# A two-layer mixer and expert kernel: scaled triangles and decay differences on ScalarE, an own region for the boundary factors, two weight items ahead of the transposes back, and another order at the start of the queries

## The chip, the cores and the metric

The kernel runs on one core of a Trainium2 chip. The metric is the device time of one execution in microseconds (us), median of several runs. The engines are PE (TensorE), VectorE (DVE), ScalarE (ACT), Pool (GpSimd) and SP (SyncE, which here only issues weight transfers).

## The reference, cut to what matters

Two blocks follow each other on x of 256 tokens by 1024 features. Each has a mixer and then a retrieval over 16384 single-neuron experts, of which every token takes 16 for each of 8 heads. The change is in the second block's mixer and at the start of both retrievals:

```
proj = _rmsnorm(x, norm1) @ w_in          # a_q a_k a_v a_beta a_alpha a_gate b_f b_i b_q b_gate g_a g_b
qkv  = silu(causal_conv(a_q, a_k, a_v))
beta = sigmoid(a_beta);  g = -exp(a_log) * softplus(a_alpha + dt_bias)
G = cumsum(g);  decay = where(causal, exp(G_i - G_j), 0)
lhs = eye + tril((k*beta) @ k^T * decay, -1)      # solved, unit diagonal
a_qk = (q @ k^T) * decay                          # o_a = gated delta rule
f_gate = lb + (1 - lb) * sigmoid(b_f)             # second recurrence, per-feature decay
y = sigmoid(g_a) * (o_a @ w_branch_a) + sigmoid(g_b) * (o_b @ w_branch_b);  x += y @ w_out

q = h2 @ w_pq;  s = q . sub_keys;  top 16 of each half, top 16 of the 256 sums -> expert index, gate
u = expert_u[idx]; h = gelu(x . u);  v = expert_v[idx];  x += sum(gate * h * v)
```

## The kernel before, in words

**Weights.** All weights stream as blocks of 128 x 1024 floats (512 KB) through `ring` (4 slots), in the order of `plan`. A block is two pieces of 512 columns. For each piece ScalarE writes the high part, rounded to fp32r (`ahead`, L903), then VectorE (L1283) or Pool (L2134) writes the residual; `by_pool` says which. There are six slots for split pieces (`PARTS`), so piece p waits until PE has used piece p - 6. Every engine's `ahead(n)` moves its own high-water mark by n pieces, at a place written by hand into that engine's program. PE's products are three fp32r matmuls (L357 to L359) a tile; 48 of them use four pieces and make one item (`by_feature` or `by_token`) in one of 8 PSUM banks.

**Order.** Every engine's program is written out by hand, and each engine takes its own strictly in order, with waits on semaphores. The second mixer has these stretches:

1. 12 conv items. VectorE applies the taps (L1818, L1821) and the second half of silu (L1832, L1834), ScalarE the tanh (L1152). In between step by step (`delta_gates`): the gates `beta` and `g`, the cumulated `G`, 16 triangles `TG` = triangle times g of one head (VectorE, L1796), ones times `TG` on PE (`("D", q)`, L662, four of them), the differences to `G` cut at zero (VectorE, L1802), the exponential (ScalarE, L1145) and the masking with the triangle (VectorE, L1807).
2. Item `ag0`, the `qk` transposes (L677) and their copies, then items `ag1` to `ag3` on PE while VectorE takes the sums of squares (L1858, L1860), ScalarE their root (L924) and VectorE scales q, k and v (`unit`, L1869 to L1873).
3. The transposes back (`("back", c2)`, L688) and their copies, the products `L` and `Q` (L705), which VectorE multiplies with the decays (L1882, L1884), item `bf0`.
4. The triangular inverse, six levels of four groups, 24 steps: L732 and L741 on PE, VectorE and ScalarE evacuate, L697 transposes. Items `bf1`, `bf2` and `bf3` lie between the steps. The items that follow are listed in `fillers`.
5. U (L760), the gated delta output, the second recurrence, the branches' outputs, `w_out2` and the residual.

**Experts** (`experts(e, ...)`, e = 1 and 2). PE makes query items from `wq`. Item i is copied by ScalarE (L914) and multiplied with the keys (`keyed`, L581); ScalarE scales the result into S (L1034). VectorE finds a head's 16 experts in `chosen(j)` (L1556 to L1606), which gives `eidx`. Pool gathers for each of 256 k one row pair for every token (L2156, 1 MB each, 10 landing slots). VectorE forms `dot(k)` (L1630) with the normed input, which `with_gain` (L1622) writes to PSUM. ScalarE makes gelu, weight and a diagonal (L1045 to L1053), PE adds the weighted rows (L604). The keys and two rows of gains come by DMAs that Pool issues (L2146 to L2149).

Of the kernel before, what the change touches and what calls it, by code (L numbers as in the profile page):

```python
# [14 lines left out]
P = 128  # L15
# [10 lines left out]
NLEV = 7  # L26

# [51 lines left out]
def build(nc, d, out):  # L79
    ctx = ExitStack()  # L80
    with ctx:
# [142 lines left out]
        BF = region(2048, 2048, c=8)  # L224
# [11 lines left out]
        SS = region(26624, 1024, h=8)  # L236
        WT = region(27648, 1024, h=8)
# [3 lines left out]
        bkf, bff, bqf = region(10240, 2048), region(2048, 2048), region(4096, 2048)  # L241
        BB, BFs, bb = spare[:, :].rearrange("p (s n) -> p s n", s=16), region(2048, 2048, s=16), spare[:, :]
# [88 lines left out]
        def tensor_program(pq, pe):  # L331
# [307 lines left out]
            def delta_gates():  # L639
# [16 lines left out]
                yield  # L656
                yield
                yield
                for q in range(4):
                    o = bank(("D", q))  # L660
                    pq.wait_ge(*on(("TG", 15)))
                    pe.matmul(o[:, :], ones, TG[:, 4 * q:4 * q + 4, :], start=True, stop=True).then_inc(*full(("D", q)))  # L662
                    yield
# [45 lines left out]
            def items():  # L709
                for name, i in fillers:  # L710
                    if name in ("bf", "bq"):
                        yield by_feature, (name, i), "w_in2", "n1"
                    elif name == "ya":
                        yield by_token_whole, (name, i), "wa", "oT", oT
                    else:
                        yield by_token, (name, i), "w_in2", "n1"
            left = items()

            def item():
                kind, *a = next(left)  # L720
                kind(*a)

# [170 lines left out]
        def scalar_program(aq, ac):  # L893
# [229 lines left out]
            def delta_gates():  # L1123
                copy(region(8192, T)[0:16], pb[place["ab"]][0:16, 0:T], "ab")
                yield
                abp = pb[place["abT"]][:, 0:32].rearrange("p (t n) -> p t n", t=2)
                aq.wait_ge(*full("abT"))
                ac.activation(v2(sv["beta"]), abp[:, :, 0:8], ACT.Tanh, scale=0.5).then_inc(*up("a_delta", "beta_tanh"))
                aq.wait_ge(*on("alpha_min"))
                ac.activation(sv["t2"], sv["t2"], ACT.Exp).then_inc(*up("a_delta", "alpha_exp"))  # L1130
                aq.wait_ge(*on("alpha_one"))
                ac.activation(sv["t2"], sv["t2"], ACT.Ln).then_inc(*up("a_delta", "alpha_ln"))
                aq.wait_ge(*on("ld_rows"))
                ac.activation(small[:, 320:328], r_alog, ACT.Exp).then_inc(*up("a_delta", "a_exp"))
                yield
                yield
                aq.wait_ge(*on("G_left"))
                ac.activation(sv["kd"], sv["kd"], ACT.Exp).then_inc(*up("a_delta", "kd"))
                ac.activation(sv["eG"], sv["G"], ACT.Exp).then_inc(*up("a_delta", "eG"))
                yield  # L1140
                yield
                for _ in range(4):
                    yield
                aq.wait_ge(*on(("taken", ("D", 3))))
                ac.activation(DT, DT, ACT.Exp).then_inc(*up("a_delta", "D_exp"))  # L1145

            def conv_tanh(i):
                aq.wait_ge(*on(("conv", i)))
                if i >= 4:
                    aq.wait_ge(*on(("silu", i - 4)))  # L1150
                tm = tmpc[:, (i % 4) * 512:(i % 4 + 1) * 512].rearrange("p (c t) -> p c t", c=2)
                ac.activation(tm, CT[:, 2 * i:2 * i + 2, :], ACT.Tanh, scale=0.5).then_inc(*up("a_conv", ("conv_tanh", i)))  # L1152

            gate_steps = delta_gates()
            for i in range(12):
                ahead(4)
                if i:
                    conv_tanh(i - 1)
                next(gate_steps, None)
            conv_tanh(11)  # L1160
            for _ in gate_steps:
                pass
            ahead(4)
            copy(AG[:, :, 0:T], half(("ag", 0)), ("ag", 0))
            for n, (g, t) in enumerate((g, t) for g in range(6) for t in range(NT)):
                if n % 2 == 0:
                    copy(QK[:, t, 4 * g:4 * g + 4, :], bank4(("qk", g, t)), ("qk", g, t))
            ahead(4)
            copy(AG[:, :, T:2 * T], half(("ag", 1)), ("ag", 1))
            root(nrm, "unit")  # L1170
            for i in range(2, 4):
                ahead(4)
                copy(AG[:, :, i * T:(i + 1) * T], half(("ag", i)), ("ag", i))
            for c2 in range(0, 12, 2):
                copy(CT[:, 2 * c2:2 * c2 + 2, :], half(("back", c2)), ("back", c2))
            aq.wait_ge(*on("lb_less"))
            ac.activation(p2, p2, ACT.Exp).then_inc(*up("a_lb", "lb_exps"))
            for i in range(4):
                aq.wait_ge(*on(("taken", ("ag", i))))
            ac.activation(gate_a, AGf, ACT.Tanh, scale=0.5).then_inc(*up("a_tanh", "ag_tanh"))  # L1180

# [23 lines left out]

            item()
# [3 lines left out]
            for n, (lev, g) in enumerate(steps):  # L1210
                if (4 * lev + g) % 8 == 7:
                    item()
# [60 lines left out]
        def vector_program(vq, ve):  # L1273
# [266 lines left out]
            def experts(e, wq):  # L1540
# [123 lines left out]
                ahead(4)  # L1664
# [98 lines left out]
            def delta_gates():  # L1763
# [30 lines left out]
                vq.wait_ge(*on("g"))  # L1794
                for s in range(16):
                    ve.tensor_scalar(TG[:, s, :], triu, sv["g"][:, s:s + 1], None, ALU.mult).then_inc(*up("v_delta", ("TG", s)))  # L1796
                    if s % 8 == 7:
                        yield
                for q in range(4):
                    vq.wait_ge(*full(("D", q)))  # L1800
                    for s in range(4 * q, 4 * q + 4):
# [45 lines left out]
            for _ in gate_steps:  # L1847
                pass
# [460 lines left out]
```

## Time and profile before

| what | value |
|---|---|
| median of 3 runs | 2039.79 us (2035.16 to 2040.49) |
| the profiled execution: its time, its span | 2036.71 us, 2034.9 us |
| PE busy, mean granted clock | 1702.4 us (84%), 0.973 |
| VectorE, ScalarE, Pool busy | 1336.4 us (66%), 913.9 us (45%), 839.4 us (41%) |
| chain that ended last | PE 38%, DMA 34%, DVE 16%, ACT 8% |
| first gather of experts 1 and 2 | 180.5 us, 1369.0 us |

The span runs from the first to the last instruction. A busy time is a sum over stretches with different limits. The chain follows each wait back to what ended it, and a granted clock of 1.0 is 2.4 GHz, 0.5 is 1.2 GHz.

### The profile page before, as it was taken

Reading aid. Unit: us, or ns where it says so; the run is one execution under the profiler, and the core shown is the slowest. Engines: PE = TensorE matmul, PEld = TensorE weight load, DVE = VectorE, ACT = ScalarE, POOL = GpSimd, SP = SyncE. Lnnn points to the kernel's source line nnn. Section 1 sums busy time; section 2 is a strip of 40 time slices with the busy share of each in tenths; the row PEclk is TensorE's granted clock in tenths of the full one; section 3 lists DMA queues with packets and bytes.
Section 4 is the critical chain, followed back from the end, with each engine's and each line's share of the span. In section 5 each row is a group of like instructions: output and inputs, shape, how many; then the busy total and the mean of one; then the engine's idle time right before and its main releaser. Section 6 shows DMA issues by size and latency. Waiting matters only on the chain.

```text
span 2034.9 us, 22626 instructions
## 1 busy us (share of the span) xinstructions
PE 1702.4 (84%) x7622; PEld 1047.5 (51%) x7622; DVE 1336.4 (66%) x2922; ACT 913.9 (45%) x2366; POOL 839.4 (41%) x762
## 2 busy tenths in 40 slices
PE   8986889877887778789799989977899787777887
PEld 7985444422322222579799989973444222222222
DVE  4666776766776664499646773547776677667644
ACT  5554545444544443445324344454444444444443
POOL 4325333333333333367525465544333333333331
PEclk9998999999999999999899999989999999999999
DMA  7446999999999999543213333559999999999996
GB/s 247 129 129 267 420 421 421 422 421 421 422 421 421 421 421 422 216 135 125 73 53 101 100 112 114 167 169 421 421 421 421 421 422 422 421 422 421 421 422 286
DMA packets 102052, 637.60 MB, mean 313 GB/s; under 512 B 11264, under 2 KB 12544, under 8 KB 36144
## 3 DMA queue, kind: packets, MB, share of 16 engines
q0 software_dynamic: 75216, 543.73, 64.3%
q1 hardware_dynamic: 26720, 92.43, 14.1%
q8 instruction: 60, 0.98, 0.2%
q14 instruction: 56, 0.46, 0.1%
HBM read 635.07 MB, written 1.05 MB: 313 GB/s over the span
## 4 chain that ended last, share of the span: by engine, by line
PE 38%; DMA 34%; DVE 16%; ACT 8%; issue 3%; POOL 0%; SPq 0%; DVEq 0%; ACTq 0%
DMA arena<-in_uv,arena 29%; PE pb L604 19%; DMA spare<-in_uv,arena 4%; PE pb L357 4%; PE pb L358 4%; PE pb L359 4%; ACT arena L1053 3%; DVE arena L1630 3%; PE pb L430 1%; PE pb L741 1%; ACT parts L903 1%; PE pb L732 1%; DVE arena L1821 1%; DVE parts L1283 1%; DMA arena<-in_sk 1%
## 5 line engine op out<-in xcount | busy, mean ns | idle before, releaser
L604 PE MATMUL pb<-arena 128*128 128x512 f32 x1848 | 910.2, 622 | 223.9 <-ACT arena L1053 222.0
L1630 DVE SCALAR_TENSOR_TENSOR arena<-arena,pb 128x1024 f32<-128x1024 f32 x462 | 563.3, 1219 | 375.2 <-DMA arena<-in_uv,arena 375.2
L2156 POOL DMA_INDIRECT arena<-in_uv,arena x462 | 438.3, 949 | 734.0 <-PE pb L604 681.9
L604 PEld LDWEIGHTS pb<-arena 128*128 128x128 f32 x1848 | 321.8, 192 | 779.3 <-ACT arena L1053 511.3
L2134 POOL TENSOR_TENSOR parts<-ring,parts 128x512 fp32r<-128x512 f32 x228 | 340.1, 1510 | 346.3 <-ACT parts L903 344.0
L1045 ACT ACTIVATE arena<-arena 128x1 f32<-128x1 f32 x512 | 103.3, 202 | 621.7 <-DVE arena L1630 567.3
L903 ACT ACTIVATE parts<-ring 128x512 fp32r<-128x512 f32 x328 | 197.8, 627 | 198.8 <-PE pb L359 183.2
L1053 ACT ACTIVATE arena<-cst,arena 128x128 f32<-128x128 f32 x512 | 205.5, 401 | 48.7 <-ACT arena L1048 1.1
L357 PE MATMUL pb<-xl,parts 128*128 128x256 f32 x704 | 221.6, 315 | 4.1 <-DVE xl L1315 2.6
L358 PE MATMUL pb<-xh,parts 128*128 128x256 f32 x704 | 201.3, 286 | 0.0
L359 PE MATMUL pb<-xh,parts 128*128 128x256 f32 x704 | 201.1, 286 | 0.0
L357 PE MATMUL pb<-parts,xh 128*128 128x256 f32 x608 | 176.7, 291 | 14.2 <-DVE parts L1283 9.6
L358 PE MATMUL pb<-parts,xl 128*128 128x256 f32 x608 | 174.2, 287 | 0.0
L359 PE MATMUL pb<-parts,xh 128*128 128x256 f32 x608 | 174.1, 286 | 0.0
L1048 ACT ACTIVATE arena<-arena 128x1 f32<-128x1 f32 x512 | 150.8, 294 | 19.3 <-ACT arena L1045 0.4
L1283 DVE TENSOR_TENSOR parts<-ring,parts 128x512 fp32r<-128x512 f32 x100 | 78.2, 791 | 104.3 <-ACT parts L903 104.1
L357 PEld LDWEIGHTS pb<-xl,parts 128*128 128x128 f32 x704 | 137.2, 195 | 16.4 <-issue 13.8
L358 PEld LDWEIGHTS pb<-xh,parts 128*128 128x128 f32 x704 | 137.3, 195 | 10.8 <-issue 10.8
L359 PEld LDWEIGHTS pb<-xh,parts 128*128 128x128 f32 x704 | 136.9, 195 | 0.0
L357 PEld LDWEIGHTS pb<-parts,xh 128*128 128x128 f32 x608 | 118.9, 196 | 15.1 <-DVE parts L1283 10.0
L358 PEld LDWEIGHTS pb<-parts,xl 128*128 128x128 f32 x608 | 119.0, 196 | 0.0
L604 PE MATMUL pb<-spare,arena 128*128 128x512 f32 x200 | 99.6, 621 | 23.2 <-ACT arena L1053 23.1
(297 smaller groups left out, 1779.2 us busy)
## 6 DMA issues: line engine op xcount, KB each, us to landing
ring<-in_w_in SPq DMA_DIRECT2D x108, 512.0 KB, 3.5
ring<-in_wq SPq DMA_DIRECT2D x32, 512.0 KB, 6.1
ring<-in_w_out SPq DMA_DIRECT2D x16, 512.0 KB, 3.6
arena<-in_uv,arena POOLq DMA_INDIRECT x462
ring<-in_wa SPq DMA_DIRECT2D x8, 512.0 KB, 3.4
ring<-in_wb SPq DMA_DIRECT2D x8, 512.0 KB, 3.8
arena<-in_sk POOLq DMA_DIRECT2D x2, 1024.0 KB, 6.3
arena<-in_tail POOLq DMA_DIRECT2D x1, 1280.0 KB, 11.3
```

The costliest lines, as they stand in the source:

```text
L357: pe.matmul(o, lh, rl, start=start, stop=False, skip_group_check=True)
L358: pe.matmul(o, ll, rh, start=False, stop=False, skip_group_check=True)
L359: return pe.matmul(o, lh, rh, start=False, stop=stop, skip_group_check=True)
L604: ins = pe.matmul(ys[hf][:, :], diags[:, k % 4, :], lands[k % LANDS][:, D + hf * 512:D + (hf + 1) * 512], start=k % (8 * K) == 0, stop=k % ...
L903: ac.activation(split(p)[0], raw(p), ACT.Copy).then_inc(*up("a_hi", ("hi", p)))
L1045: ac.activation(acted[:, k:k + 1], hidden[:, k:k + 1], ACT.Gelu).then_inc(*up("a_gelu", ("gelu", e, k)))
L1048: ac.activation(weight_of[:, k:k + 1], acted[:, k:k + 1], ACT.Copy, scale=gate[:, k:k + 1]).then_inc(*up("a_weight", ("weight", e, k)))
L1053: ac.activation(diags[:, k % 4, :], ident, ACT.Copy, scale=weight_of[:, k:k + 1]).then_inc(*up("a_diag", ("diag", e, k)))
L1283: ve.tensor_tensor(lo, raw(p), hi.bitcast(F32), ALU.subtract).then_inc(*up("v_lo", ("lo", p)))
L1630: ve.scalar_tensor_tensor(z, z, 1.0, xg[t], ALU.mult, ALU.mult, accum_out=hidden[:, k:k + 1]).then_inc(*up("v_dot", ("dot", e, k)))
L2134: gp.tensor_tensor(lo, raw(p), hi.bitcast(F32), ALU.subtract).then_inc(*up("g_lo", ("lo", p)))
L2156: gp.indirect_dma_start(lands[k % LANDS], None, rows_uv, bass.IndirectOffsetOnAxis(ap=eidx[:, k:k + 1], axis=0)).then_inc(*up(f"dma_rows{k ...
```

## The change

- The 16 triangles are made by ScalarE (`ACT.Copy` with a scale pointer), in four portions of the conv loop. The four D matmuls move from the conv loop to behind `ag1`. ScalarE reads the differences from PSUM as relu(G - D), in two batches (`decay_gaps`), and the exponential has scale -1. The root for `unit` stands behind the second batch and the copy of `ag2`, the exponential behind it. The masking multiply stands behind VectorE's copies of the transposes back.
- `BF` has a region of its own, apart from `CT`; `SS`, `WT`, `EX[0]` and `KW[1]` get other places.
- `EARLY = 2` items (`bf0`, `bf1`) go ahead of the transposes back, on all engines. The small constants of the lower bound (L1890 to L1900) and their exponential move into the end of the conv stretch. In the inverse one item is left (`n == 7`). Pool makes the four `silu` of the gate behind three items.
- Queries: VectorE splits 6 instead of 8 pieces ahead, runs `chosen(0)`, then `with_gain(0)` and `gates(0)`, then splits 6 instead of 4. Pool's mark ahead of the keys' DMA stands two pieces earlier.

```diff
+EARLY = 2
-        BF = region(2048, 2048, c=8)
+        BF = region(26624, 2048, c=8)
-        SS = region(26624, 1024, h=8)
-        WT = region(27648, 1024, h=8)
+        SS = region(28672, 1024, h=8)
+        WT = region(29696, 1024, h=8)
-        EX = [region(2048, 2048), region(30720, 2048)]
+        EX = [region(26624, 2048), region(30720, 2048)]
-        KW = [region(20480, 2048), region(26624, 2048)]
+        KW = [region(20480, 2048), region(2048, 2048)]
...
 # tensor_program
             for i in range(1, 4):
                 by_token(("ag", i), "w_in2", "n1")
+                if i == 1:
+                    for q in range(4):
+                        o = bank(("D", q))
+                        pq.wait_ge(*on(("TG", 15)))
+                        pe.matmul(o[:, :], ones, TG[:, 4 * q:4 * q + 4, :], start=True, stop=True).then_inc(*full(("D", q)))
+            for _ in range(EARLY):
+                item()
             for c2 in range(12):
...
-                if (4 * lev + g) % 8 == 7:
+                if n == 7:
                     item()
...
 # scalar_program
+                for s in range(16):
+                    ac.activation(TG[:, s, :], triu, ACT.Copy, scale=sv["g"][:, s:s + 1]).then_inc(*up("a_delta", ("TG", s)))
+                    if s % 4 == 3:
+                        yield
+            def decay_gaps(qs):
+                for q in qs:
+                    aq.wait_ge(*full(("D", q)))
+                    for s in range(4 * q, 4 * q + 4):
+                        ins = ac.activation(DT[:, s, :], pb[place["D", q]][:, (s % 4) * P:(s % 4 + 1) * P], ACT.Relu,
+                                            bias=sv["G"][:, s:s + 1], scale=-1.0)
+                    ins.then_inc(*taken(("D", q)))
...
             copy(AG[:, :, T:2 * T], half(("ag", 1)), ("ag", 1))
+            decay_gaps((0, 1))
+            ahead(4)
+            decay_gaps((2, 3))
+            copy(AG[:, :, 2 * T:3 * T], half(("ag", 2)), ("ag", 2))
             root(nrm, "unit")
-            for i in range(2, 4):
-                ahead(4)
-                copy(AG[:, :, i * T:(i + 1) * T], half(("ag", i)), ("ag", i))
+            for q in range(4):
+                aq.wait_ge(*on(("taken", ("D", q))))
+            ac.activation(DT, DT, ACT.Exp, scale=-1.0).then_inc(*up("a_delta", "D_exp"))
+            ahead(4)
+            copy(AG[:, :, 3 * T:4 * T], half(("ag", 3)), ("ag", 3))
+            for _ in range(EARLY):
+                item()
...
 # vector_program: the loops of L1796 and L1802 are gone, L1807 stands behind the copies of the transposes back
-                ahead(8)
-                with_gain(0)
+                ahead(12 - PARTS)
                 for _ in chosen(0):
                     pass
+                with_gain(0)
                 gates(0)
-                ahead(4)
+                ahead(PARTS)
...
 # gpsimd_program
-            ahead(18 * 4)
+            ahead(18 * 4 - PARTS + 4)
...
-                ahead(8)
+                ahead(PARTS - 4 + 8)
                 ahead(8 * 4 - PARTS - 8)
...
-            item()
-            silu(0)
-            silu(1)
-            item()
-            silu(2)
-            silu(3)
-            for _ in range(len(fillers) - 2):
+            for _ in range(EARLY + 1):
                 item()
-            ahead(8 * 4)
+            for q in range(4):
+                silu(q)
+            for _ in range(len(fillers) - EARLY - 1):
+                item()
+            ahead(8 * 4 - PARTS + 4)
```

## Rows read from the trace of the kernel before

**Rows 1.** The page, the chain that ended last: shares of the span by engine.
```profile
PE 38%; DMA 34%; DVE 16%; ACT 8%; issue 3%; POOL 0%; SPq 0%; DVEq 0%; ACTq 0%
```

**Rows 2.** DMA busy tenths in 40 slices; then busy by window (PE, PEld, DVE, ACT, POOL; PEclk, DMA, GB/s).
```profile
DMA  7446999999999999543213333559999999999996
...
190.00:200.00 10.00, 9.59 (x24) 4.45 (x25) 9.58 (x33) 2.78 (x10) 5.62 (x6) 0.73 1.01 424
```

**Rows 3.** Timelines and chain, run-up to experts 1: start, duration, instruction, [idle before <-releaser].
```profile
153.41 2.52 POOL L2134 TENSOR_TENSOR parts<-ring,parts 128x512 fp32r<-128x512 f32 x2 [9.48 <-ACT parts L903]
...
155.87 6.18 DMA arena<-in_sk
...
160.17 0.60 ACT L914 ACTIVATE arena<-pb 128x512 f32<-128x512 f32 x1 [0.42 <-PE pb L359]
...
162.09 1.16 PE pb L581 x8
...
163.35 0.84 ACT L1034 ACTIVATE arena<-pb,small 128x256 f32<-128x256 f32 x2 [2.06 <-PE pb L581]
...
168.78 0.69 DVE L1283 TENSOR_TENSOR parts<-ring,parts 128x512 fp32r<-128x512 f32 x1 [10.40 <-ACT parts L903]
...
172.13 0.48 DVE L1556 MAX8 arena<-arena 128x8 f32<-128x128 f32 x2
...
180.49 1.53 POOL L2156 DMA_INDIRECT arena<-in_uv,arena  x1 [12.33 <-DVE arena L1606]
```

**Rows 4.** Timelines and chain, the same places of experts 2.
```profile
1347.01 0.60 ACT L914 ACTIVATE arena<-pb 128x512 f32<-128x512 f32 x1 [0.39 <-PE pb L359]
...
1349.10 2.07 PE pb L581 x8
...
1360.68 0.48 DVE L1556 MAX8 arena<-arena 128x8 f32<-128x128 f32 x2
```

**Rows 5.** Groups by line, VectorE, 869 to 947: count | busy, mean ns | idle before.
```profile
L1796 DVE TENSOR_SCALAR arena<-cst,small 128x128 f32<-128x128 f32 x16 | 9.5, 664 | 0.0
...
L1802 DVE TENSOR_SCALAR arena<-pb,small 128x128 f32<-128x128 f32 x16 | 4.5, 338 | 0.0
L1807 DVE TENSOR_TENSOR arena<-arena,cst 128x2048 f32<-128x2048 f32 x1 | 2.3, 2293 | 0.4 <-ACT arena L1145 0.4
```

**Rows 6.** PE's waits in the mixer, 860 to 1345: total, times, longest.
```profile
PE pb L688 <- DVE arena L1873: 9.3, 1, 9.3
PE pb L662 <- DVE arena L1796: 7.4, 1, 7.4
```

**Rows 7.** Chain and timelines, second mixer up to the masked products.
```profile
845.57 0.63 ACT xh L1108 x2
...
903.44 0.86 PE pb L662 x2
...
950.40 0.69 DVE L1294 COPY arena<-pb 128x512 f32<-128x512 f32 x1 [0.55 <-PE pb L677]
...
960.42 0.23 ACT L924 ACTIVATE small<-small 128x32 f32<-128x32 f32 x1 [1.85 <-DVE small L1303]
...
961.25 17.93 POOL L2134 TENSOR_TENSOR parts<-ring,parts 128x512 fp32r<-128x512 f32 x8 [1.00 <-ACT parts L903]
...
976.97 7.15 PE pb L688 x48
...
986.21 0.69 DVE L1882 TENSOR_TENSOR arena<-pb,arena 128x512 f32<-128x512 f32 x1 [1.38 <-PE pb L705]
```

**Rows 8.** The chain in the inverse: start, duration, instructions.
```profile
1002.43 1.14 PE pb L732 x8
...
1032.47 0.45 PE pb L697 x4
...
1038.66 0.89 PE pb L732 x8
...
1072.94 3.63 PE pb L760 x32
```

More of the change, by code:

```diff
@@ L655, in delta_gates, with items, item @@
                 pe.matmul(o[:, 16:32], ones, sv["g"], start=True, stop=True).then_inc(*full("G"))
[L656 to L663, printed above, removed]
+            def items():
+                for name, i in fillers:
+                    if name in ("bf", "bq"):
+                        yield by_feature, (name, i), "w_in2", "n1"
+                    elif name == "ya":
+                        yield by_token_whole, (name, i), "wa", "oT", oT
+                    else:
+                        yield by_token, (name, i), "w_in2", "n1"
+            left = items()
+            def item():
+                kind, *a = next(left)
+                kind(*a)
             gate_steps = delta_gates()
@@ L707, in tensor_program @@
                     ins.then_inc(*full((which, g)))
[L709 to L721, printed above, removed]
             item()
@@ L1121, in scalar_program @@
             ahead(PARTS - 4)
[L1123 to L1145, printed above, removed]
@@ L1174, in scalar_program @@
[L1174 to L1180, printed above, removed]
             def evacuate(key):
@@ new lines, in scalar_program @@
+            gate_steps = delta_gates()
+            for i in range(12):
+                ahead(4)
+                if i:
+                    conv_tanh(i - 1)
+                next(gate_steps, None)
+            conv_tanh(11)
+            aq.wait_ge(*on("lb_less"))
+            ac.activation(p2, p2, ACT.Exp).then_inc(*up("a_lb", "lb_exps"))
+            for _ in gate_steps:
+                pass
+            ahead(4)
+            copy(AG[:, :, 0:T], half(("ag", 0)), ("ag", 0))
+            for n, (g, t) in enumerate((g, t) for g in range(6) for t in range(NT)):
+                if n % 2 == 0:
+                    copy(QK[:, t, 4 * g:4 * g + 4, :], bank4(("qk", g, t)), ("qk", g, t))
@@ new lines, in scalar_program @@
+            ahead(4)
+            copy(AG[:, :, T:2 * T], half(("ag", 1)), ("ag", 1))
+            decay_gaps((0, 1))
+            ahead(4)
+            decay_gaps((2, 3))
+            copy(AG[:, :, 2 * T:3 * T], half(("ag", 2)), ("ag", 2))
+            root(nrm, "unit")
+            for q in range(4):
+                aq.wait_ge(*on(("taken", ("D", q))))
+            ac.activation(DT, DT, ACT.Exp, scale=-1.0).then_inc(*up("a_delta", "D_exp"))
+            ahead(4)
+            copy(AG[:, :, 3 * T:4 * T], half(("ag", 3)), ("ag", 3))
@@ L1206, in scalar_program @@
+            for _ in range(EARLY):
+                item()
+            for c2 in range(0, 12, 2):
+                copy(CT[:, 2 * c2:2 * c2 + 2, :], half(("back", c2)), ("back", c2))
+            for i in range(4):
+                aq.wait_ge(*on(("taken", ("ag", i))))
+            ac.activation(gate_a, AGf, ACT.Tanh, scale=0.5).then_inc(*up("a_tanh", "ag_tanh"))
             item()
@@ new lines, in vector_program @@
+            at["unit"] = on(("unit_vb", 1))
+            ahead(8)
+            for _ in range(EARLY):
+                item()
+            for c2 in range(1, 12, 2):
+                copy(CT[:, 2 * c2:2 * c2 + 2, :], half(("back", c2)), ("back", c2))
+            vq.wait_ge(*on("D_exp"))
+            ve.tensor_tensor(DT, DT, bm(triu, 16), ALU.mult).then_inc(*up("v_delta", "decay"))
+            vq.wait_ge(*on("decay"))
+            for g in range(4):
+                vq.wait_ge(*full(("L", g)))
+                ve.tensor_tensor(LT[:, g], bank4(("L", g)), DTg[:, g], ALU.mult).then_inc(*taken(("L", g)))
+                vq.wait_ge(*full(("Q", g)))
+                ve.tensor_tensor(AQ[:, g], bank4(("Q", g)), DTg[:, g], ALU.mult).then_inc(*taken(("Q", g)))
+                vq.wait_ge(*on(("taken", ("L", g))))
+                ve.copy_predicated(LT[:, g], bm(ident.bitcast(U32), 4), bm(ones, 4)).then_inc(*up("v_inverse", ("M", g)))
+                vq.wait_ge(*on(("M", g)))
+                ve.tensor_tensor(XT[:, g], LT[:, g], bm(signs[0], 4), ALU.mult).then_inc(*up("v_inverse", ("XT", 0, g)))
```

146 lines of the change are left out of this document (60 added, 86 removed).

## The prediction

> **What bounds the kernel now.** I read the chain of work that ended last first. Its shares are PE 38%, DMA 34%, DVE 16%, ACT 8% [rows 1]: no engine bounds the whole kernel, so I cut it into stages. In the two expert stages the DMA engines are busy to nine tenths or more in every slice, and the share is 1.01 with 424 GB/s ten us after the first gather [rows 2]: the stages last as long as their bytes, and only an earlier first gather can shorten them. Everything between them (the second mixer) and the run-up to each first gather is a chain of engines, read from the timelines, the chain and the waits.
>
> Run-up, experts 1 [rows 3]: Pool is idle from 143.9 on. Its next two residuals (wq pieces 4 and 5) wait 9.48 us for ScalarE's high parts until 153.41, and the keys' DMA stands behind them at 155.87. PE has query 0 copied at 160.77 (160.17 + 0.60) but can multiply by the keys only at 162.09. ScalarE then writes S by 164.2. VectorE should start `chosen(0)` there, yet its queue holds `ahead(8)`, whose last two pieces (12, 13) are VectorE's own: it waits 10.40 us and starts the top-k at 172.13. First gather: 180.49. Experts 2 has the same pattern: query copied at 1347.61, keys product at 1349.10, top-k at 1360.68 [rows 4].
>
> Mixer: VectorE runs from 869 to 946 with almost no idle, and 16.3 us of that are the scaled triangles (L1796, 9.5), decay differences (L1802, 4.5) and the masking multiply (L1807, 2.3) [rows 5]. PE's two longest waits in the mixer are for these: 7.4 us at L662, the decay matmul, and 9.3 us at L688, the transposes back, for the unit scaling [rows 6].
>
> **The change, part by part.** *Query order.* Pool stops its high-water mark two pieces earlier (pieces 0 to 3 of wq are none of its own), so the three DMAs go out at about 143.9 instead of 155.87. The four other residuals follow as their high parts come: 1.8 us of DMA issue is hidden in the 9.48 us idle. The keys take 6.2 us (162.09 - 155.87), so they are there at 151 and the product waits only for the query: 160.8 + 1.16 = 162.0, plus one ScalarE evacuation of 0.84: S at 162.9. VectorE now splits up to piece 11 only, all Pool's, so it waits for nothing. `chosen(0)` starts at 162.9 instead of 172.13: **9.2 us**. `with_gain(0)`, moved behind it (1.4 us), and the six residuals (0.69 each less overlap, 3.7 us) fall between the gather's issue and its landing: 5.1 us there, with the keys' DMA of the same 1 MB at 6.2. ScalarE's `exps(0)` also gets free earlier. Pool's other residuals had ended 12.33 us before the first gather, at 168.2, which is still ahead of the new first gather (180.49 - 9.2 = 171.3). Experts 2: the query at 1347.61, a product of 1.2 us (2.07 at the slow clock [rows 4]), S at 1349.7 instead of a start at 1360.68: **11.0 us**. Against both: one weight block of 512 KB that was loaded before the first gather now lies inside the saturated stage, 0.52 MB / 421 GB/s = 1.2 us each. Net **8.0 and 9.8**. These carry through whole, because DMA is saturated soon after the first gather and to the last one [rows 2].
>
> *Conv stretch.* VectorE loses 16.3 us; with the 0.4 us wait at L1807 that is the upper bound. PE bounds from the other side: it loses the 7.4 us wait, the four decay matmuls (4 x 0.86 = 3.4 [rows 7]) and the slow clock behind the wait (at least another 0.86, with part of the next item some 2.7): 13.5. VectorE worked through eleven convs in 74 us with the 16.3 us in them: 5.3 to 5.6 us for one without them, where PE needs 5.74 [rows 8]. So both keep step. VectorE gets the six small bound constants in front of its copies (about 1.2 us, before at 997). I take **12.4 us** earlier at the end of the `qk` transposes: VectorE's last copy at 938.7 instead of 951.1 [rows 7]. The 16 triangles on ScalarE: two activations 128x128 with a scale pointer took 0.63 [rows 7], so 0.31 each, 5.0 us in four portions of 1.25 beside four high parts and a tanh of at most 0.63 each, 3.2 of 5.7 us: hidden. At 0.6 each, 2.4 a conv, they would just fit.
>
> *Unit stretch.* Here a wait is made. The unit root now stands in ScalarE's queue behind ag1, eight differences, the split for `ag3`, eight differences and the copy of `ag2`. PE: `ag1` 937.9 to 943.7, D matmuls 3.4 to 947.1, `ag2` to 953.0. ScalarE: split 0.5, eight differences 2.6 (0.33 each; the nearest row is again 0.31 [rows 7]; bounds 0.2, the 128x32 root, and 0.6, the 128x512 copy [rows 3, 7]), copy 0.55, table load and root 1.5 (an estimate of 1.3 for the load): root at 958.1 against 960.65 before [rows 7]. VectorE has its sums of squares at 948 and stands idle for 10 us. The second half of the unit scaling is 15.6 us beside a busy Pool: unit ready at 974.4, from 976.97. Behind the root stand the decay exponential (table load 1.3 + 1.9) and then the split of pieces 66 to 69, which the early items `bf0` and `bf1` need. Pool then needs 2.2 us a piece beside VectorE (17.93 us for 8 [rows 7], against 1.26 alone [rows 3]) where PE uses one in 1.47. Six pieces from 961.9 on end at about 975, so `bf1` ends at 976.1, later than unit. So the transposes back start at 976.1 instead of 976.97, but warm: 48 x 0.11 = 5.3 us (0.45 for four in the inverse [rows 8]) instead of 7.15 [rows 7]. The copies end 2.7 us earlier, and the moved masking multiply (2.3) costs part of it again: the masked products start at 984.3 instead of 986.2 [rows 7]. PE goes on with L and Q, `bf2` and the first turn without a gap, where before it waited 2.6 us for ScalarE: level 1 starts at 997.4 instead of 1002.43 [rows 8], **5.0 us**.
>
> *Inverse.* Before there are three items between the levels, afterwards one. One item is 5.74 us (1032.92 to 1038.66 [rows 8]); **11.5 us** off. The steps themselves, (1072.94 - 1002.43 - 17.2) / 24 = 2.2 us, are PE back to back.
>
> *At nothing:* new regions for BF, SS, WT, EX and KW change no instruction; the reordered Pool gates have until VectorE's use after the inverse (some 50 us of cover; uncovered 8 us).
>
> One rule speaks against moving this work. The rows give 32 x 0.31 = 10 us on ScalarE against 14 us on VectorE under Pool's load. The Trainium skill (ScalarE: Activation LUTs, Rules for kernel authors) says to use VectorE for relu and multiply. Its cost formula (What ACT_TABLE_LOAD costs) would give about 0.29 us each back to back, 9.4 us in all as an estimate, which agrees with the rows on the price. The rule would matter only if ScalarE became the late engine, which is the first rival below.
>
> **Sum.** 8.0 + 5.0 + 11.5 + 9.8 = 34.3 us. Against the profiled execution's own 2036.7 this gives 2002.4. The median of the three runs is 3.1 us above that execution and the lowest 1.5 below, so I put the median at **2004**.
>
> **Rivals.** (A) *ScalarE becomes the late engine.* If a difference read from PSUM costs 0.6 us, root, exponential and the split of piece 66 come 4 to 5 us later, PE stands longer ahead of the transposes and they run slow. The 5.0 term becomes -1 or so: 2010. For it: ScalarE's queue is in order and already was the last to be ready at level 1. Against: in this stretch it mostly waits, 1.85 us for VectorE's sums just ahead of the root [rows 7]. By the Trainium skill's rule this is what one would expect. (B) *The earlier gathers are not carried through*, because the first ones wait for something else (diag, gates, the weight splits): 17.8 us less, 2021. Against: the share of 1.01 from 10 us after the first gather [rows 2]. (C) *Less contention than I charge.* VectorE's idle in the unit stretch lets Pool run ahead; unit and bf1 end 5 to 6 us earlier and so does all behind them: 1998. (D) *Slower:* PE's granted clock stays at 1.2 GHz through the transposes back, L, Q, `bf2` and the inverse, about 80 us of work at 2.4 GHz. Each us of it at 1.2 GHz costs one; beyond 34 the change loses, all of it would cost 80: 2084. For it: the transposes back ran slow behind the wait. Against: PE idles less than before, and in the inverse it took 0.89 us for L732 where the first one, behind a wait, took 1.14 [rows 8]. (E) *The constants or the moved decay matmuls eat the conv gain,* as PE and VectorE meet at the banks: 8 us less, 2012, inside the range.
>
> **Chances.** Forecast with E's milder forms 0.55, A 0.14, B 0.10, C 0.15, D 0.03, nothing visible or a smaller loss 0.03. The range from C with its neighbours to past A, 1993 to 2017, leaves out B, D and the last: 0.16 to 0.2. A difference under 0.3% (6 us) could not be told from none. Faster 0.93, same 0.03, slower 0.04.
>
> **What would show it.** The first gather 9 us after the new S, VectorE without a wait for ScalarE's high parts ahead of the top-k; keys' DMA near 144 and 1331. No wait of PE at the decay matmul. A new wait of VectorE of about 10 us for the root, and PE waiting in `bf0`/`bf1` for Pool's residuals. Inverse 59 us long instead of 70.5. The prediction is wrong if the first gather moves by less than 7 us, if the gather stage gets longer than by 2 us, or if the transposes back start later than 980.

## The result, and the profile after

The changed kernel takes 2011.21 us (median of four executions, 2007.68 to 2012.7) where the kernel before, beside it on the same chip, takes 2038.34 (2035.16 to 2040.49): ratio 0.9866, 95% interval 0.9846 to 0.9885, so about 27 us faster. The prediction was 2004 with 1993 to 2017. The profiled execution of the changed kernel took 2011.54, with a span of 2009.7; the two spans differ by 25.2. One execution of q_only and one of lb_moved, kernels of the experiments below, were far slower than the others (5212 and 2104 us) and are left out of the medians.

The page of the changed kernel: the chain's shares by engine, and the DMA busy tenths in 40 slices [rows 1, 2].

```profile
DMA 36%; PE 36%; DVE 16%; ACT 8%; issue 3%; POOL 1%; SPq 0%; DVEq 0%; ACTq 0%
...
DMA  6437999999999999654303333569999999999996
```

The gather stages are as full as before, and what lies between them is shorter. Pool now has 1% of the chain; that is one place, ahead of the transposes back, shown below.

Positions in the two traces can't be subtracted as they stand: ScalarE's copy of query 0 of experts 1, ahead of which nothing was changed, begins at 160.17 before and at 163.24 after, and among the runs of this study anywhere from 158.1 to 163.2. I measure each stage from its own start. "Diagonals" stands for ScalarE's last diagonal matrix of experts 1, at 837.14 before and 834.27 after, which is the start of the mixer.

| stretch | before | after | gain | predicted |
|---|---|---|---|---|
| query 0 to first gather, experts 1 | 20.32 | 12.68 | 7.6 | 9.2 |
| first gather to diagonals | 656.65 | 658.35 | -1.7 | -1.2 |
| diagonals to the end of the `qk` transposes | 113.22 | 104.91 | 8.3 | 12.4 |
| diagonals to level 1 of the inverse | 165.29 | 164.24 | 1.05 | 5.0 |
| inverse | 70.34 | 59.05 | 11.3 | 11.5 |
| end of inverse to query 0, experts 2 | 274.24 | 272.33 | 1.9 | 0 |
| query 0 to first gather, experts 2 | 22.03 | 12.37 | 9.7 | 11.0 |
| first gather of experts 2 to the end | 665.86 | 667.44 | -1.6 | -1.2 |

The third row lies inside the fourth. The others sum to 28.3; less the 3.1 by which query 0 itself came later this is the 25.2. The 1.9 between the inverse and query 0 is variation: the ten kernels of the experiments below show 274.3 to 275.2 there. The gain of 1.05 up to level 1 is uncertain in the same way: q_only, q_vector and q_pool below have the mixer of before and take 165.6 to 167.4 for the stretch, mix_only has the changed one and takes 164.6, so it is 1 to 3 us.

The run-up to experts 1 after the change, timelines of Pool, ScalarE and VectorE and two pieces of the chain [rows 3]:

```profile
145.71 1.30 POOL L2140 TENSOR_TENSOR parts<-ring,parts 128x512 fp32r<-128x512 f32 x1 [4.30 <-ACT parts L903]
146.95 0.76 POOL L2152 DMA_DIRECT2D arena<-in_sk  x1
...
156.48 2.52 POOL L2140 TENSOR_TENSOR parts<-ring,parts 128x512 fp32r<-128x512 f32 x2 [7.72 <-ACT parts L903]
...
163.24 0.60 ACT arena L914
...
163.98 1.15 PE pb L582 x8
...
166.51 0.49 DVE L1572 MAX8 arena<-arena 128x8 f32<-128x128 f32 x2 [5.06 <-ACT arena L1034]
...
167.36 2.67 POOL L2140 TENSOR_TENSOR parts<-ring,parts 128x512 fp32r<-128x512 f32 x2 [0.50 <-ACT parts L903]
...
168.87 1.44 DVE L1585 TENSOR_TENSOR arena<-arena 128x256 f32<-128x256 f32 x1
...
175.92 1.25 POOL L2162 DMA_INDIRECT arena<-in_uv,arena  x1 [5.89 <-DVE arena L1622]
```

The keys' DMA is issued at 146.95, ahead of Pool's 7.72 us wait for high parts instead of behind it, and the product waits for nothing but the copied query. VectorE now waits 5.06 us for S itself (L1034), no longer 10.40 for a high part. The top-k (from its first MAX8 to the gather) lasts 9.4 us instead of 8.36: Pool's last two residuals run beside it, and the 128x256 sum of pairs takes 1.44 us where it took 0.41 before.

In experts 2 it is the same, with 1.27 us for a 128x32 conversion that takes 0.17 in experts 1 [rows 4]:

```profile
1329.89 0.60 ACT L914 ACTIVATE arena<-pb 128x512 f32<-128x512 f32 x1 [0.39 <-PE pb L360]
...
1332.80 0.49 DVE L1572 MAX8 arena<-arena 128x8 f32<-128x128 f32 x2 [4.67 <-ACT arena L1034]
...
1334.01 2.73 POOL L2140 TENSOR_TENSOR parts<-ring,parts 128x512 fp32r<-128x512 f32 x2 [0.45 <-ACT parts L903]
...
1335.51 1.27 DVE L1588 CAST arena<-arena 128x32 f32<-128x32 uint32 x1
...
1342.26 1.25 POOL L2162 DMA_INDIRECT arena<-in_uv,arena  x1 [5.51 <-DVE arena L1622]
```

The conv stretch. First the waits of PE in the mixer up to the inverse [rows 6], then VectorE's groups by line and shape (count | busy, mean ns | idle before), two of the kernel before from 856 to 951 and those of the changed kernel from 859 to 940 [rows 5]:

```profile
PE pb L358 <- POOL parts L2140: 4.7, 5, 1.7
PE pb L684 <- ACT arena L914: 2.7, 1, 2.7
PE pb L684 <- DVE arena L1310: 2.6, 1, 2.6
```

```profile
L1834 DVE TENSOR_TENSOR arena<-arena 128x512 f32<-128x512 f32 x12 | 17.0, 1421 | 0.4
...
L1832 DVE TENSOR_SCALAR arena<-arena 128x512 f32<-128x512 f32 x12 | 9.5, 790 | 0.0
```

```profile
L1836 DVE TENSOR_TENSOR arena<-arena 128x512 f32<-128x512 f32 x12 | 19.1, 1593 | 0.4
L1834 DVE TENSOR_SCALAR arena<-arena 128x512 f32<-128x512 f32 x12 | 10.1, 841 | 0.0
...
L1847 DVE TENSOR_TENSOR small<-cols 128x8 f32<-128x8 f32 x1 | 1.3, 1254 | 0.0
L1854 DVE TENSOR_TENSOR small<-small 128x8 f32<-128x8 f32 x1 | 1.2, 1229 | 0.0
L1860 DVE TENSOR_TENSOR small<-small 128x8 f32<-128x8 f32 x1 | 1.2, 1185 | 0.0
L1858 DVE TENSOR_TENSOR small<-small 128x8 f32<-128x8 f32 x1 | 1.0, 953 | 0.0
L1856 DVE RECIPROCAL small<-small 128x8 f32<-128x8 f32 x1 | 0.2, 202 | 0.0
```

Both long waits of before, for the triangles and for the unit scaling, are gone; the new one is for Pool's residuals. The 16.3 us of triangles, differences and mask are gone from VectorE too, but the six bound constants cost 5.0 us there, 0.16 to 0.20 each before and four of them about 1.2 now. In the kernel before the silu's multiplications of the same kind (its L1834 and L1832) took 17.0 and 9.5 us; they now take 2.7 us more. Most of it is two of the twelve two-input multiplications: one takes 0.69 us with no instruction of Pool beside it and 1.65 to 1.75 us beside one, and in the changed kernel one runs free of Pool where in the kernel before three did. 16.7 (the 16.3 and the 0.4 us wait at L1807) less 5.0 less 2.7 is 9.0, and the stretch got 8.3 shorter. The constants also stand ahead of VectorE's copies of the transposes, and PE waits twice for such copies (2.7 and 2.6 us) where it waited once before (2.6).

The unit stretch, timelines and, of the instructions at 962.86 and 977.47, the chain [rows 7]:

```profile
949.03 0.18 DVE L1319 TENSOR_SCALAR small<-small 128x32 f32<-128x32 f32 x1
...
954.86 2.15 ACT L1175 ACTIVATE arena<-pb,small 128x128 f32<-128x128 f32 x8
...
957.51 1.28 ACT L924 ACT_TABLE_LOAD   x1
958.81 0.23 ACT L924 ACTIVATE small<-small 128x32 f32<-128x32 f32 x1
...
959.07 0.35 DVE L1323 RECIPROCAL small<-small 128x32 f32<-128x32 f32 x1 [9.86 <-ACT small L924]
...
962.86 11.43 POOL parts L2140 x5
...
970.85 2.30 DVE L1921 TENSOR_TENSOR arena<-arena,small 128x1024 f32<-128x1024 f32 x1
...
977.47 5.25 PE pb L702 x48
...
983.36 2.28 DVE L1930 TENSOR_TENSOR arena<-arena,cst 128x2048 f32<-128x2048 f32 x1
```

VectorE has its sums at 949 and waits 9.86 us for the root; the unit scaling is done at 973.1, but the transposes back wait behind `bf1` until 977.3, and `bf0` and `bf1` wait for Pool: its first five residuals for them take 11.43 us, 2.3 us each, beside VectorE's unit scaling. The transposes take 5.4 us instead of 7.15.

### The profile page after: what moved, and what is told of

The parts are those of the page before. It is cut to its first block, busy times and chain, and to the rows that moved or that the text cites. A ratio compares the mean times of both kernels' runs of the same rounds, so it can differ in the third digit from the quotient of the medians.

```text
span 2009.7 us, 22627 instructions
## 1 busy us (share of the span) xinstructions
PE 1697.9 (84%) x7622; PEld 1042.5 (52%) x7622; DVE 1335.7 (66%) x2890; ACT 922.3 (46%) x2398; POOL 840.1 (42%) x762
## 3 DMA queue, kind: packets, MB, share of 16 engines
HBM read 635.07 MB, written 1.05 MB: 317 GB/s over the span
## 4 chain that ended last, share of the span: by engine, by line
DMA 36%; PE 36%; DVE 16%; ACT 8%; issue 3%; POOL 1%; SPq 0%; DVEq 0%; ACTq 0%
DMA arena<-in_uv,arena 33%; PE pb L605 17%; PE pb L358 4%; PE pb L360 4%; PE pb L359 4%; DVE arena L1646 3%; ACT arena L1053 3%; DMA spare<-in_uv,arena 3%; PE pb L431 1%; DVE arena L1823 1%; PE pb L741 1%; DVE arena L1836 1%; PE pb L732 1%; DVE parts L1299 1%; ACT arena L1048 1%
## 5 line engine op out<-in xcount | busy, mean ns | idle before, releaser
L358 PE MATMUL pb<-xl,parts 128*128 128x256 f32 x704 | 219.8, 312 | 10.3 <-POOL parts L2140 4.7
L358 PE MATMUL pb<-parts,xh 128*128 128x256 f32 x608 | 176.6, 290 | 14.2 <-DVE parts L1299 9.6
L358 PEld LDWEIGHTS pb<-xl,parts 128*128 128x128 f32 x704 | 137.1, 195 | 22.4 <-issue 16.0
L358 PEld LDWEIGHTS pb<-parts,xh 128*128 128x128 f32 x608 | 118.3, 194 | 15.3 <-DVE parts L1299 10.0
```

Source lines behind the costliest of these rows:

```text
L358: pe.matmul(o, lh, rl, start=start, stop=False, skip_group_check=True)
```

## The experiments

Ten kernels, each timed beside the kernel before.

| kernel | median us | ratio | 95% interval |
|---|---|---|---|
| q_only | 2025.66 | 0.9936 | 0.9916 to 0.9956 |
| q_vector | 2027.75 | 0.9948 | 0.9932 to 0.9965 |
| q_pool | 2035.15 | 0.998 | 0.9971 to 0.999 |
| mix_only | 2024.59 | 0.9934 | 0.9917 to 0.995 |
| lb_moved | 2007.08 | 0.9826 | 0.9784 to 0.9867 |
| exp_late | 2011.51 | 0.9855 | 0.9818 to 0.9891 |
| root_early | 2007.57 | 0.9835 | 0.9799 to 0.9872 |
| all3 | 2002.42 | 0.9811 | 0.9774 to 0.9848 |
| early0 | 2019.88 | 0.991 | 0.9893 to 0.9926 |
| tri_vector | 2016.28 | 0.9887 | 0.987 to 0.9903 |

The median of the kernel before was 2038.92 beside the first four, 2039.05 beside the next four, 2038.65 beside the last two, and 2038.34 beside the changed kernel. As these agree within 0.8 us, I compare kernels with each other by their medians. The executions of one kernel lie 1 to 7 us apart, so where two kernels differ by 3 or 4 us I give the traces' difference beside it.

**q_only: the query order alone**, in the kernel before.

```diff
-                ahead(8)
-                with_gain(0)
+                ahead(12 - PARTS)
                 for _ in chosen(0):
                     pass
+                with_gain(0)
                 gates(0)
-                ahead(4)
+                ahead(PARTS)
```

and Pool's three lines on its high-water mark, as in the change.

> The kernel before with the query order alone (VectorE's and Pool's marks, chosen(0) ahead of with_gain(0)). Theory 1: the first gathers come 7.6 and 9.7 us earlier against query 0's copy, 1.6 us of each is given back in the saturated stage, so the whole is 14 us faster (ratio 0.993). Rival: the starts carry nothing through and the gain of the whole change is the mixer's; then this is within 3 us of before.

13.3 us faster. Query 0 to the first gather is 12.68 and 12.37 us in the two run-ups, the same as in the whole change. The gain is carried to the end, so rival B is out.

**q_vector: VectorE's half of it**, and **q_pool: Pool's half.**

> VectorE's part of the query order alone; Pool still splits two pieces ahead of the keys' DMA. Theory 1: the wait for ScalarE's high parts was the costly one. The keys' product stays at its old place, S at 164.2, and the first gather comes some 6.5 to 7 us earlier; most of the 14 us, about 10 to 11. Rival: without the early keys nothing moves, since the chain passed through the keys' DMA; then 0 to 2.

> Pool's part of the query order alone; VectorE still waits for pieces 12 and 13. Theory 1: S comes 1 to 1.5 us earlier, but the top-k starts behind the same wait, which itself follows PE's item 1 and so moves by those 1 to 2 us: 1 to 3 us faster in all, and in experts 2 more than in experts 1 as PE stays warm. Rival (the keys' DMA sets the start): 12 us or more.

q_vector gains 11.2 us of the 13.3: its run-ups are 14.05 and 15.25 us long. q_pool gains 3.8, more than the 1 to 3 expected; its run-ups are 19.11 us both. VectorE still waits there for ScalarE's high part ahead of the top-k, but ScalarE comes to it 1.2 us earlier: ahead of S it waits 0.85 us for the keys' product, where it waited 2.06 [rows 3]. In experts 2 the gain is 2.9 us: it waits 0.85 instead of 3.15, and the keys' product takes 1.13 instead of 2.07 [rows 4]. In q_pool, timelines of Pool and VectorE:

```profile
143.63 0.76 POOL L2146 DMA_DIRECT2D arena<-in_sk  x1
...
167.34 0.69 DVE L1283 TENSOR_TENSOR parts<-ring,parts 128x512 fp32r<-128x512 f32 x1 [9.21 <-ACT parts L903]
...
170.68 0.48 DVE L1556 MAX8 arena<-arena 128x8 f32<-128x128 f32 x2
```

So the wait on VectorE was the main part, and the keys' DMA, which is 12 us earlier here than in [rows 3], was worth little alone. In the run-ups the halves add up: 6.3 and 1.2 us against 7.6 in experts 1, 6.8 and 2.9 against 9.7 in experts 2. By the medians they sum to 15.0 against 13.3, a difference that these runs can't tell from their spread.

**mix_only: the change without the query order.**

> The changed kernel with the query order of before. Theory 1: the mixer is 14 us shorter from PE's first feature matmul to query 0 of experts 2, of it 11.4 in the inverse; 12 to 14 us faster in all, and with q_only's 14 this adds up to the whole change. Rival: the two parts overlap (one hides the other), and the sum is off by over 5 us.

14.3 us faster. With q_only's 13.3 that is 27.6, where the whole change gains 27.1: no overlap of the two halves can be seen.

**lb_moved: the bound constants out of the contended place.** The first two go ahead of the conv stretch, the last four behind `mean("unit", ...)`, where VectorE waits for the root.

```diff
+            # ahead of the convs, behind row_final(1)
+            ve.tensor_tensor(lbc, c_lb[:, 0, :], c_lb[:, 1, :], ALU.max)
+            ve.tensor_tensor(p2, c_lb, bm(lbc, 2), ALU.subtract)
...
             mean("unit", nrm, 1.0)
+            ve.tensor_tensor(oml, p2[:, 0, :], p2[:, 1, :], ALU.add)
+            ve.reciprocal(oml, oml)
+            ve.tensor_tensor(lbc, p2[:, 0, :], oml, ALU.mult)
+            ve.tensor_tensor(oml, p2[:, 1, :], oml, ALU.mult)
             inverse_root("unit", nrm)
```

> The changed kernel, with the first two bound constants computed by VectorE at the mixer's start and the other four in its idle time ahead of the unit root. Theory 2: in the changed kernel these six small instructions take 5.0 us at the end of the conv stretch, because those with two inputs take about 1.2 us each beside a busy Pool instead of 0.17; the qk transposes end 3.5 to 4 us earlier and all behind them too: 3 to 4 us faster than the changed kernel. Rival: the root, which waits for PE, or Pool's residuals set the start of the transposes back anyway, and under 1 us arrives.

2007.08, 4.1 us below the changed kernel's median. In the profile the stretch from the diagonals to the end of the `qk` transposes is 102.3 us instead of 104.91, and level 1 comes 2.65 earlier. The last four, in their new place, with Pool at rest from 945.85 on (VectorE's timeline of lb_moved):

```profile
945.93 0.16 DVE L1903 TENSOR_TENSOR small<-small 128x8 f32<-128x8 f32 x1
946.12 0.20 DVE L1905 RECIPROCAL small<-small 128x8 f32<-128x8 f32 x1
946.36 0.17 DVE L1907 TENSOR_TENSOR small<-small 128x8 f32<-128x8 f32 x1
946.56 0.17 DVE L1909 TENSOR_TENSOR small<-small 128x8 f32<-128x8 f32 x1
```

The three with two inputs are the same to the element as in the changed kernel and take a sixth to an eighth of the time. There Pool was at work beside them (its timeline in the changed kernel):

```profile
930.17 5.38 POOL L2140 TENSOR_TENSOR parts<-ring,parts 128x512 fp32r<-128x512 f32 x4 [4.73 <-ACT parts L903]
```

The first two did not get away from Pool at the mixer's start (VectorE's and Pool's timelines of lb_moved):

```profile
843.31 11.75 POOL L2140 TENSOR_TENSOR parts<-ring,parts 128x512 fp32r<-128x512 f32 x9 [1.19 <-ACT parts L903]
...
847.55 1.26 DVE L1779 TENSOR_TENSOR small<-cols 128x8 f32<-128x8 f32 x1
848.84 1.23 DVE L1781 TENSOR_TENSOR small<-cols,small 128x16 f32<-128x16 f32 x1
```

They cost 2.5 us there, so of the 5.0 us about 2.5 are saved, which is what the stretch shows.

**exp_late: the decay exponential between the two early items' evacuations** instead of ahead of the split for `ag3` and both of them.

```diff
-            ac.activation(DT, DT, ACT.Exp, scale=-1.0)
             ahead(4)
             copy(AG[:, :, 3 * T:4 * T], half(("ag", 3)), ("ag", 3))
-            for _ in range(EARLY):
-                item()
+            item()
+            ac.activation(DT, DT, ACT.Exp, scale=-1.0)
+            item()
```

> The changed kernel with ScalarE's decay exponential (3.1 us with its table load) behind the evacuation of bf0 instead of ahead of the split of pieces 66 to 69. Theory 3: the early items end late because those splits stand behind the root and the exponential; bf1 ends 2.5 to 3 us earlier, and the transposes back start with it, unit (973.1) becoming the bound 4 us earlier: 2 to 3 us faster than the changed kernel. Rival: Pool's own rate of 1.7 us a piece beside VectorE is the bound, so it gains 0 to 1.

2011.51: no difference from the changed kernel, as the rival had it. In the profile PE waits 3.2 us for Pool instead of 4.7 and the transposes back start 1.6 earlier, but level 1 only 0.65. The exponential's place is worth less than these runs can tell.

**root_early: the unit root ahead of the second half of the differences and the split for `ag3`.**

```diff
             decay_gaps((0, 1))
+            root(nrm, "unit")
             ahead(4)
             decay_gaps((2, 3))
             copy(AG[:, :, 2 * T:3 * T], half(("ag", 2)), ("ag", 2))
-            root(nrm, "unit")
```

> The changed kernel with the unit root behind the first batch of differences. VectorE's 9.9 us wait goes and unit is ready at some 966 instead of 973.1. Theory 3: PE is held by bf0 and bf1, not by unit, so only the lesser contention of Pool is won: 0 to 2.5 us. Rival (rival A of the prediction in another form, the late root costs its own length): 4 us or more, the full distance to where PE would stand.

2007.57, 3.6 us below the changed kernel; level 1 comes 3.9 earlier. All its six executions are shorter than all six of exp_late, which were timed beside them. I had expected 0 to 2.5, since I held Pool to be slow beside VectorE wherever VectorE works. Waits of VectorE and of PE, 940 to 985:

```profile
DVE small L1323 <- ACT small L924: 0.6, 1, 0.6
```

```profile
PE pb L358 <- POOL parts L2140: 1.3, 3, 0.5
```

With VectorE's work done earlier, Pool is free for `bf0` and `bf1` and PE waits 1.3 us for it instead of 4.7. Of Pool's first six residuals behind the exponential, which the two items need, four take 2.3 to 3.3 us in the changed kernel, beside the unit scaling; here two take 2.3 and four 1.3 to 1.5. So the 10 us that VectorE stands idle in the changed kernel were not only idle: they pushed its work onto the time in which PE needs Pool.

**all3: the three edits together.**

> The three edits together. Theories 2 and 3: 6 to 9 us faster than the changed kernel, 33 or so faster than before, with the transposes back starting at PE's own pace (no wait for Pool over 1 us in bf0 and bf1). Rival: a next limit at once, under 4 us.

2002.42, 8.8 us below the changed kernel, where the single ones gave 4.1, 0 and 3.6. In the profile level 1 comes 9.35 us earlier, against 2.65, 0.65 and 3.9 (7.2) in the single ones. The surplus lies ahead of the end of the `qk` transposes, where all3's code is lb_moved's: 5.4 us shorter than in the changed kernel instead of 2.6. Of it 1.3 us is there at the last silu: a one-input conversion at the mixer's start took 0.21 us, and 1.38 beside Pool in lb_moved's profile, and PE's wait behind it (L358) is 0.2 us instead of 1.5. This is the fastest version of the study: 36.6 us below the kernel before.

**early0: no weight items ahead of the transposes back.**

```diff
-EARLY = 2
+EARLY = 0
...
-                if n == 7:
+                if n in (3, 11, 19):
```

> From the changed kernel (2011 us): no weight item stands ahead of the transposes back; bf0 and bf1 go back into the inverse, so it holds three items between its levels again (behind the same steps as before). Everything else stays. Theory 1 (the items fill time in which TensorE waits anyway, at the price that the transposes start some 4 us later, at the clock they find): TensorE stands from the end of ag3 to the unit scaling, the transposes back start 3 to 5 us earlier than in the changed kernel and take 7 us instead of 5.4, the inverse is 70.3 us long instead of 59.05. 11.3 - 4 + 1.7: 7 to 10 us slower, 2019 to 2021. Theory 2 (the early items only move work, since TensorE waits in them for Pool's residuals as long as it would wait for the unit scaling): 0 to 3 us slower, 2011 to 2014.

2019.88, 8.7 us above the changed kernel. PE's waits, 940 to 985:

```profile
PE pb L702 <- DVE arena L1921: 13.2, 1, 13.2
```

The transposes back start 4.0 us earlier and run slow again (7.2 us), level 1 comes 2.2 earlier, and the inverse is 70.32 us long. 11.3 less 2.2 is 9.1. PE's 13.2 us wait is what the two early items fill: 11.5 us of work for 2.2 of delay.

**tri_vector: the scaled triangles back on VectorE.**

```diff
-                    ac.activation(TG[:, s, :], triu, ACT.Copy, scale=sv["g"][:, s:s + 1])
+                    ve.tensor_scalar(TG[:, s, :], triu, sv["g"][:, s:s + 1], None, ALU.mult)
```

> From the changed kernel (2011 us): the 16 scaled triangles go back to VectorE (two portions of eight between the convs, where they were before); the differences stay on ScalarE, the decay matmuls behind ag1. Theory 1 (VectorE is the later engine of the conv stretch and has no slack beside TensorE): the triangles cost there what they cost before, 9.5 us, less what VectorE had to wait for TensorE; the qk transposes end 7 to 9.5 us later, and all behind them too: 7 to 10 us slower, 2018 to 2021. Theory 2 (my prediction's bound: TensorE sets the stretch once the decay wait is gone, VectorE has a few us of slack): 3 to 6 us slower, 2014 to 2017. Theory 3 (ScalarE would have been no better a place, as the Trainium skill's rule to keep plain multiplies on VectorE suggests): within 2 us, 2009 to 2013.

2016.28, 5.1 us above the changed kernel. The time falls into the range of theory 2, but its mechanism doesn't hold: in the changed kernel VectorE waits nowhere for PE from the second conv to the last silu. VectorE's groups, 856 to 943:

```profile
L1835 DVE TENSOR_TENSOR arena<-arena 128x512 f32<-128x512 f32 x12 | 17.2, 1431 | 0.4
L1806 DVE TENSOR_SCALAR arena<-cst,small 128x128 f32<-128x128 f32 x16 | 9.6, 670 | 0.0
L1833 DVE TENSOR_SCALAR arena<-arena 128x512 f32<-128x512 f32 x12 | 9.5, 794 | 0.0
```

The `qk` transposes end 5.8 us later than in the changed kernel, for 9.6 us of triangles. Level 1 comes 6.2 later. 2.5 of the difference is the silu's multiplications, which are back at the kernel before's duration, and 1.1 is the first bound constant (0.15 instead of 1.25): with the triangles in between three of the twelve two-input multiplications run free of Pool, as in the kernel before, and not one. So it was not PE that gave VectorE slack; what VectorE sheds it partly loses again beside Pool. No run moves the differences or the mask by themselves.

## Why the prediction was right, and where its terms were off

The time alone would fit rivals A (2010) and E (2012) better than the 2004 of the forecast; it is the stages that show which steps held.

**Query order, 8.0 and 9.8 predicted, 5.9 and 8.1 net in the traces.** The mechanism is as told: q_only shows it alone and whole. Two sizes were off. From the query's copy to the top-k it takes 3.27 us where I had 2.73, since I left out the hand-over from ScalarE to VectorE (0.41 in the chain). And I gave the top-k its old 8.36 us: with Pool's last residuals moved beside it by my own reckoning, it is 9.4. The stages lengthen by 1.7 and 1.6 where I charged 1.2 for the weight block; what the rest is, no run shows. The first gather moved by 7.6 us against query 0, over the 7 that I had named as the least; in the traces' own time it moved by 4.6 (180.49 to 175.92), since query 0 came 3.1 later. That VectorE's half would be most of it was not said in the prediction; the runs show it.

**Conv stretch, 12.4 predicted, 8.3 measured. This is the term that was most in error.** The terms on the other engines held: no wait of PE at the decay matmul, and four triangles on ScalarE take 1.27 us, 0.32 each, hidden. Two terms of VectorE's side were mis-sized. The bound constants were priced at 1.2 us by their rows of before, where Pool rested, and take 5.0 beside a busy Pool; lb_moved gets 2.6 us back. And the silu's multiplications, taken as unchanged, lose 2.7 us more to Pool; tri_vector shows that they take their old time once the triangles are back. "Both keep step" held as a rate: from the fourth conv on PE ends an item every 5.76 us and VectorE takes 5.65 for a conv. PE came out as reckoned too, 12.0 us earlier at the end of `ag0` for my 13.5, although VectorE's first tap came 1.2 us later than before. But VectorE works 6 to 8 us behind PE from the gates at the second conv on, so what it meets at the end of the stretch, the constants, comes on top. Rival E named the loss at this place (8 us of it at the worst), though for the banks, not for Pool.

**Unit stretch: the steps were right, the 5.0 went with the conv term.** From VectorE's last `qk` copy to level 1 I had 58.7 us (from its end at 938.7 to 997.4) and the trace shows 58.6 (939.91 to 998.51). VectorE's wait for the root was to be about 10 us and is 9.86; eight differences 2.6 and take 2.15; the transposes back 5.3 and take 5.4; PE was to wait for Pool's residuals and does so five times, 4.7 us in all. All of it stands 4 us late because the conv stretch ends 4 us late. In the time of the kernel before, shifted by the diagonals' 2.9 us, the transposes back start at 980.2, just over the 980 that I had named as the bound. What the prediction did not see is that the wait it foretold had a price that a reordering could save: root_early shows 3.6 us.

**Inverse, 11.5 predicted, 11.3 measured.** One item of 5.74 us less twice. early0 gives the other side of it: 70.32 us with three items.

**The rivals.** A is refuted: a difference from PSUM costs 0.27 us, not 0.6, and tri_vector, with the triangles on VectorE, is slower by 5 us. The rule of the Trainium skill (ScalarE: Activation LUTs, Rules for kernel authors) to use VectorE for multiplies, which it grounds on a bf16 rate, does not hold for these fp32 triangles: ten of the sixteen triangles took 0.27 to 0.28 us on VectorE, with Pool at rest or beside it for 0.23 us at most, but six took 1.29 to 1.33 beside it, 0.67 in the mean, and on ScalarE they took 0.32 (ScalarE's timeline of the changed kernel).

```profile
882.89 1.27 ACT L1166 ACTIVATE arena<-cst,small 128x128 f32<-128x128 f32 x4
```

What A said about the queue, though, was true in part: the root's place in ScalarE's queue did cost time. B is refuted by q_only. C did not come: Pool was no help during VectorE's idle time, since its own input, ScalarE's high parts, stands behind the same queue. D did not come: the granted clock is 0.99 from 939 to 977 and 1.00 up to the end of the inverse (windows of the changed kernel; columns as in [rows 2]).

```profile
939.00:977.00 38.00, 33.32 (x247) 30.42 (x247) 27.64 (x17) 22.11 (x43) 26.78 (x16) 0.99 0.27 85
977.00:998.00 21.00, 20.12 (x178) 19.91 (x178) 18.69 (x25) 9.43 (x15) 11.02 (x9) 1.00 0.34 103
998.00:1057.00 59.00, 57.03 (x513) 56.39 (x511) 31.99 (x56) 12.59 (x29) 14.40 (x14) 1.00 0.11 35
```

**The sum.** 34.3 predicted, 28.3 in the profile by stages (1.9 of it variation), 27 in the medians. The shortfall is 4.0 in the conv term (2 to 4 with the variation of the stretch named above), 3.8 in the two query terms, and 0.2 in the inverse, with the 1.9 of variation against it. In the conv term and in the top-k the error is the same: when I moved work off a queue I took the durations of what stayed as fixed.

Left open: 1.5 us of all3's surplus, behind the last silu, which no run takes apart; and how far 8.8 us against a sum of 7.7 is more than spread.

## What to carry to other kernels

When work is taken off one of two engines that get in each other's way, price what stays there again: its rows of before were measured with other neighbours. When a wait is made on purpose on an engine that seems to have time, ask what the work behind the wait will then collide with; here a 10 us idle time cost 4 us through a third engine. And of an independent item put in front of a wait, compare what it fills (13.2 us) with what it delays (4.0 at the transposes, 2.2 at level 1) before asking whether it is free.

## What the runs showed of the hardware

A two-input VectorE instruction of 8 columns took 0.95 to 1.25 us beside Pool's running 128x512 subtractions and 0.15 to 0.17 beside a resting Pool, a reciprocal with one input 0.20 in both. What is added hardly depends on the size: up to 1.1 us at 8 columns, 1.0 at 256 (0.41 to 1.44) and 1.0 at 512 (0.69 to 1.66). It is as if VectorE's instruction waited for Pool's (1.25 to 1.75 us each) to end: the constant that began at 924.21 ended at 925.46, Pool's subtraction at 925.44. The Trainium skill (SBUF — State Buffer, Terms) says this of the port pair that the two engines share: it is held for a whole instruction, and the loser is blocked. These rows agree. Instructions with one input can be slowed as well: in the changed kernel a 128x32 conversion took 1.27 us beside Pool and 0.17 elsewhere, the triangles on VectorE 1.3 and 0.27, and the silu's one-input scaling of 128x512 takes 0.42 alone and 0.84 in the mean of its twelve. Pool pays too: its subtraction takes 1.28 us alone and 2.3 to 3.3 beside the unit scaling's multiplications of 128x1024 and 128x2048.

ScalarE did a 128x128 relu with a bias pointer from PSUM in 0.27 us each, eight in a row, and a multiplication of the same size from SBUF with a scale pointer in 0.32, four in a row.
